# Running sums of squares on GpSimd instead of VectorE, in a decoder layer

## The reference

```python
def rms_norm(x, g):
    y = xf * lax.rsqrt(jnp.mean(xf * xf, axis=-1, keepdims=True) + EPS)
    return (y * g.astype(jnp.float32)).astype(x.dtype)

x = x + rms_norm(mix @ p["w_out"], p["g_post_mix"])
h = rms_norm(x, p["g_pre_x"])
qx = (h @ p["w_xq"]).reshape(B, T, N_XHEADS, XHEAD_DIM)
...
x = x + rms_norm(ox @ p["w_xo"], p["g_post_x"])
h = rms_norm(x, p["g_pre_ffn"])
...
x = x + rms_norm(f @ p["w_down"], p["g_post_ffn"])
```

## Time and profile before

| | |
|---|---|
| device time, median of 3 | 1866.59 us (1866.09 to 1868.44) |
| profiled execution, span | 1869.1 us (no other time of it is given) |
| PE / PEld busy | 94% / 87% |
| DVE / ACT / POOL busy | 61% / 47% / 0% |
| adds of Sy (line 2016) | 63, median 525 ns |
| adds of Sx (line 2023) | 42, median 518 ns |
| ACT's squares SQx waiting for the add of Sx | 27.8 us, 13 times |
| PE waiting for the add of Sx | 7.3 us, 3 times |

### The profile page before, as it was taken

The page is one execution under the profiler, slowest core; times in us unless marked ns, Lnnn a source line. Parts: engine busy times, 40 slices in busy tenths (PEclk is TensorE's granted clock), DMA queues, the critical chain, the costliest instruction groups (busy, mean ns, idle before and its releaser), DMA issues.

```text
span 1869.1 us, 30727 instructions
## 1 busy us (share of the span) xinstructions
PE 1761.3 (94%) x12286; PEld 1628.3 (87%) x12286; DVE 1133.8 (61%) x2091; ACT 875.7 (47%) x1648; POOL 0.9 (0%) x10
## 2 busy tenths in 40 slices
PE   7999999788997788999999899999999999999998
PEld 7999999455655688998877889999999999999998
DVE  5499993454674667743446766764467543576633
ACT  7322231233567465654545645543454543555533
POOL 0000000000000000000000000000000000000000
PEclk9999999899999899999999999999999999999999
DMA  7232122334322154544353333444444544444543
GB/s 236 57 121 80 59 92 92 142 119 159 120 78 93 49 159 129 158 149 128 121 156 115 100 114 115 137 140 133 141 136 141 156 132 139 139 137 144 148 137 102
DMA packets 349220, 233.76 MB, mean 125 GB/s; under 512 B 7979, under 2 KB 322465, under 8 KB 349071
## 3 DMA queue, kind: packets, MB, share of 16 engines
q1 hardware_dynamic: 342907, 220.24, 39.0%
q10 hardware_dynamic: 6172, 11.55, 1.7%
HBM read 220.68 MB, written 11.50 MB: 124 GB/s over the span
## 4 chain that ended last, share of the span: by engine, by line
PE 83%; DVE 8%; ACT 6%; issue 3%; DMA 1%; ACTq 0%; SPq 0%; DVEq 0%
PE bank L1144 77%; PE bank L1141 6%; DVE wlo L1721 1%; ACT whi L574 1%; DVE op_lo L1708 1%; DVE Y L1708 1%; DVE XT L2035 1%; ACT wide L588 1%; DVE Sx L2023 1%; ACT KTS L730 0%; ACT Pp L753 0%; DVE op_x L2038 0%; DMA cached<-in_cache_win_v_dram 0%; DVE KTS L1907 0%; DVE Sy L2016 0%
## 5 line engine op out<-in xcount | busy, mean ns | idle before, releaser
L1144 PE MATMUL bank<-op_hi,whi 128*128 128x352 f32 x1632 | 543.1, 333 | 21.7 <-DVE op_lo L1708 16.6
L1144 PE MATMUL bank<-op_hi,wlo 128*128 128x352 f32 x1632 | 528.6, 324 | 0.0
L1144 PE MATMUL bank<-op_lo,whi 128*128 128x352 f32 x1632 | 528.1, 324 | 0.0
L1721 DVE TENSOR_TENSOR wlo<-raw,whi 128x1024 fp32r<-128x1024 f32 (+1 forms) x312 | 373.3, 1199 | 245.8 <-ACT whi L574 245.2
L574 ACT ACTIVATE whi<-raw 128x1024 fp32r<-128x1024 f32 (+1 forms) x312 | 324.9, 1044 | 291.4 <-PE bank L1144 104.2
L1144 PEld LDWEIGHTS bank<-op_hi,whi 128*128 128x128 f32 x1632 | 310.5, 190 | 32.1 <-issue 26.2
L1144 PEld LDWEIGHTS bank<-op_lo,whi 128*128 128x128 f32 x1632 | 311.4, 191 | 0.5
L1144 PEld LDWEIGHTS bank<-op_hi,wlo 128*128 128x128 f32 x1632 | 310.1, 190 | 0.0
L1144 PE MATMUL bank<-fhi,whi 128*128 128x352 f32 x528 | 171.1, 324 | 0.0
L1144 PE MATMUL bank<-fhi,wlo 128*128 128x352 f32 x528 | 170.7, 323 | 0.0
L1144 PE MATMUL bank<-h1hi,whi 128*128 128x352 f32 x480 | 157.0, 327 | 3.0 <-DVE h1lo L1708 3.0
(11 more groups left out here) (277 smaller groups left out, 2369.2 us busy)
## 6 DMA issues: line engine op xcount, KB each, us to landing
raw<-in_w_up_dram SPq DMA_DIRECT2D x132, 512.0 KB, 3.8
raw<-in_w_down_dram SPq DMA_DIRECT2D x48, 512.0 KB, 3.6
raw<-in_w_out_dram SPq DMA_DIRECT2D x24, 512.0 KB, 3.7
raw<-in_w_xq_dram SPq DMA_DIRECT2D x24, 512.0 KB, 3.7
raw<-in_w_xo_dram SPq DMA_DIRECT2D x24, 512.0 KB, 3.7
raw<-in_w_in_dram SPq DMA_DIRECT2D x20, 512.0 KB, 3.8
raw<-in_w_down_dram SPq DMA_DIRECT2D x24, 384.0 KB, 3.2
cached<-in_cache_win_k_dram SPq DMA_DIRECT2D x8, 1024.0 KB, 5.4
```

The costliest lines, as they stand in the source:

```text
L1144: return pe.matmul(out, lhsT, rhs, start=first, stop=last)
L1721: dve.tensor_tensor(wlo[v % SLOTS][:, 0:nk, :], raw[v % SLOTS][:, 0:nk, :], whi[v % SLOTS][:, 0:nk, :].bitcast(F32), ALU.subtract).then_in ...
```

## The change

Both helpers move from VectorE's program to GpSimd's, with the waits and marks they have. GpSimd runs through the slots and issues in each first the add of Sy and then the adds of Sx. The places in VectorE's order where they stood are dropped.

```diff
     @block.gpsimd
@@ -559,6 +559,37 @@
         pool.memset(U[:, :, 0:PAD], 0.0).then_inc(*mark("pads", 0))
+
+        def add_y(name, c, m):
+            if m:
+                pool.wait_ge(*at("sqy", (name, c, m)))
+                if m > 1:
+                    pool.wait_ge(*at("ysum", (name, c, m - 1)))
+                pool.tensor_tensor(Sy[:, :], Sy[:, :], SQy[:, :], ALU.add).then_inc(*mark("ysum", (name, c, m)))
+
+        def add_x(name, c, m):
+            if m:
+                pool.wait_ge(*at("sqx", (name, c, m)))
+                if m > 1:
+                    pool.wait_ge(*at("xsum", (name, c, m - 1)))
+                pool.tensor_tensor(Sx[:, :], Sx[:, :], SQx[m % 2][:, :], ALU.add).then_inc(*mark("xsum", (name, c, m)))
+
+        def x_sums(t):
+            for name, c, s0, per, *_ in CHAINS:
+                for m in tiles(t - s0, 11, per):
+                    add_x(name, c, m)
+
+        for t in range(NX):
+            name, c, m = XU[t]
+            if name != "xq":
+                add_y(name, c, m)
+            x_sums(t)
+        for c in range(CH):
+            if c == 0:
+                for t in range(NX, NX + 2 * FT):
+                    x_sums(t)
+            for m in range(NT):
+                add_y("down", c, m)
@@ -2008,20 +2039,6 @@
-        def add_y(name, c, m):
-        ...
-        def add_x(name, c, m):
-        ...
@@ -2064,8 +2081,6 @@
         def chains_last(t):
             for name, c, s0, per, to, op_at, per_op in CHAINS:
-                for m in tiles(t - s0, 11, per):
-                    add_x(name, c, m)
@@ -2134,8 +2149,6 @@
-            if name != "xq":
-                add_y(name, c, m)
@@ -2230,7 +2243,6 @@
-                add_y("down", c, m)
```

## The result

The changed kernel takes 1880.7 us (median of 4 runs, 1879.2 to 1882.9) against 1867.5 us for the kernel before (4 runs too, one more than above): a ratio of 1.0065 (95% interval 1.0052 to 1.0077), or +12.1 us by the ratio. In the runs further down one execution of 4473 us and one of 3464 us were in a slow state and are left out. The profiled execution spans 1881.1 us, 12.0 more than before.

The account below looks back on a forecast made before the run. TensorE bounds most of the kernel, VectorE four stretches where it is about 96% full. Terms +11.8 - 0.8 + 0.4 = +11.4 us on 1866.6 gave 1878.0 us, range 1849 to 1892; slower 0.56, faster 0.34, same 0.10.

Parts of the forecast that it names:

- Part 1: Four stretches with VectorE about 96% full: removing 36 adds gives back 0.44 us each, 15.8 us; elsewhere nothing.
- the first rival: Whole kernel: GpSimd and VectorE don't disturb each other, so TensorE's stalls nearly all go; -19.7 us, 1847 us; chance 0.26.
- Part 2: On GpSimd: an add of 352 columns lasts 0.9 us, one stream at a time; at the top 1.2 us.
- Part 3: VectorE's two-operand instructions in the four nearly full stretches: each GpSimd add holds VectorE up its whole 0.9 us.
- Part 4: Four stretches with VectorE about 96% full: +16.6 us of hold, -4.8 us for ScalarE's earlier squares, together +11.8 us.
- Part 5: 1090 to 1130 us: seven adds cost +3.2 us, the 4.00 us stall before Sx goes; net -0.8 us, wlo late next.
- Part 6: Kernel's end: the last add of Sy, before the last roots, takes 0.9 us for 0.53, +0.4 us.
- Part 7: ScalarE's waits for sums from GpSimd's in-order queue: cost nothing unless an add takes over 1.3 us.
- the second rival: VectorE held only partly, 0.45 to 0.75 us an add, balance at 0.64: 1859 to 1872 us; chance 0.17.
- third rival: GpSimd too slow for its queue, over 1.3 us an add: about 10 us more, around 1877 and slower; chance 0.05.
- The signs: Adds of 0.9 us; VectorE instructions about 0.9 us longer, busy time up; XT and Y stalls +3 us each, 4.00 gone.

Follow-up runs that it names:

- One column on GpSimd: Changed kernel with each GpSimd add cut from 352 columns to one, same waits and order; 0.9907 against the kernel before, -17 us (1851.5 us).
- the extra adds: Kernel before, VectorE keeping its 105 adds, plus 105 same-size adds on GpSimd that nobody waits for; 1.0119 against the kernel before, +22 us.
- the third tile of squares: Kernel before with a third tile for squares of the residual, ScalarE waiting for sum m - 3 instead of m - 2; 0.9992, -1.5 us.
- writing-only kernel: Changed kernel with each GpSimd add replaced by three memsets, nothing read; 0.9952 against the kernel before, -9 us (1859.4 us).

## Why the prediction was right, point by point

The sign and the place are as forecast, and so is the mechanism in kind; 1878.0 lies 2.7 us from 1880.7, and +11.4 us beside +12.1. But the sum came out through errors that cancel. The hold and the credit were mis-sized and the price of the later sums was missing, so that it came this close is luck.

**Part 1, what comes back.** Right. One column on GpSimd, which takes the adds off VectorE at almost no price, gives -17 us; the first rival said -19.7.

**Part 2, the duration.** 0.9 us from the memsets' slope, 0.92 measured. But the reasoning isn't borne out. A memset of 352 columns took 0.39 us (0.37 by the slope), but a copy 0.48, where one stream at a time would give 0.64. For an add of one column, 176 and 352 the runs show 0.19, 0.55 and 0.92: 0.19 us and 2.08 ns a column, not 0.10 us and 3 x 0.77. The figure of the Trainium skill ("GPSIMD Engine Reference", section 3.1), scaled down in proportion to 0.77 us, came out too low because of the fixed 0.19. With it and the measured slope an estimate for 2048 columns is 4.45 us, close to the 4.50 that the page gives.

**Part 3, the hold.** Right in kind, shown by the extra adds (+22 us) and by the memsets (nothing lengthened). Mis-sized: taken as the whole 0.9 us, it measured 0.69 for one instruction. In the fourth stretch the means of VectorE's instructions in the changed kernel were these (line, name, count, busy us, mean ns):

```profile
L1752 DVE TENSOR_TENSOR wlo<-raw,whi 128x1024 fp32r<-128x1024 f32 x6 | 7.8, 1296 | 4.4 <-ACT whi L605 4.4
L1739 DVE SCALAR_TENSOR_TENSOR op_lo<-op_x,prm,op_hi 128x352 fp32r<-128x352 f32 x8 | 6.4, 834 | 0.0
L1739 DVE SCALAR_TENSOR_TENSOR Y<-Y,prm,Ry 128x352 f32<-128x352 f32 x8 | 6.0, 748 | 0.0
L2055 DVE TENSOR_TENSOR op_x<-XT,Rx 128x352 f32<-128x352 f32 x6 | 5.9, 1019 | 0.0
```

Before they were 1214, 577, 576 and 518 ns (the window of 1041 to 1070). The lengthening is 6 x 0.08 + 8 x 0.26 + 8 x 0.17 + 6 x 0.50 = 6.9 us for the 14 adds there. The same count gives 6.1, 5.7 and 5.1 us for the 9, 9 and 7 adds of the other three, together 23.8 us for 39 adds, 0.61 us each. Five of the 39 held nothing.

**Part 4, the sum of the full stretches.** The first term was 36 x (0.9 - 0.44) = +16.6 us; with 0.61 it is about +6. The credit of -4.8 us for ScalarE's earlier squares is wrong: the third tile of squares, which gives most of that freedom (10.8 of 27.8 us of waits for Sx stay), brought -1.5 us. ScalarE waits for XT instead.

**Part 5, the fifth stretch.** -0.8 us was forecast, and alone it measured 0.9997 (-2.4 to +1.1 us). The number holds, the reasons don't. The hold was put at 7 x 0.46 = +3.2 us, but there, in the changed kernel, VectorE's instructions grew by only 0.8 us in total for seven adds: four of these adds took 2.0 us, as a wlo got in ahead of them, and held the next wlo by only 0.19 us each. And the stall of 4.00 us doesn't go but splits in two; the new one stands behind ScalarE's root, not at wlo.

**Part 6, the end.** Only read, not tested alone: the last add took 0.93 us for 0.53, and TensorE's wait for it grew from 1.25 to 1.69 us. The down projections with all their adds moved measured no change.

**Part 7, the new waits.** This step failed, and its error makes up for those of parts 3 and 4. It said that the later sums cost nothing unless an add takes over 1.3 us. It took every add as 0.9 us, but the hold works on GpSimd too: the 42 adds of Sx took 1.35 us in the mean. And later sums cost something below that limit as well. The writing-only kernel disturbs VectorE in nothing and is still 8 us slower than the one of one column (0.9952 against 0.9907), its sums coming after 1.18 instead of 0.19 us. At the end of a chain nothing follows that could hide them: TensorE wants Sx at once, and in the changed kernel GpSimd had three adds to do, of 0.96, 0.92 and 1.72 us (1072.57 to 1076.28). There it waits 5.70 us where it waited 1.51.

The stall isn't the whole price. These windows of the writing-only kernel and of the one with one column run from the same instruction of TensorE to the same one, across one end of a chain (columns as in the earlier trace rows):

```profile
1030.68:1070.26 39.58, 33.38 (x196) 32.86 (x195) 25.66 (x44) 23.53 (x48) 15.27 (x42) 0.91 0.36 107
...
1027.16:1061.05 33.89, 30.72 (x196) 29.95 (x195) 25.66 (x44) 23.31 (x48) 5.11 (x14) 1.00 0.43 124
```

They differ by 5.7 us. One main part is the stall of 3.57 us. The other is the clock: it was granted at 1.00 throughout in the second, and at 0.91 in the first, 0.66 in the 10 us from 1056, that is partly at the lower of its two levels; for the same products TensorE is busy 2.7 us longer. The prediction has such a price in its first rival and none in its sum.

Put together from the runs: -17 us for adds taken off VectorE, +8 us for later sums, +21 us for GpSimd's reading, sum +12. The three are the steps from one whole kernel to the next, so they must add up; only the extra adds are a measurement beside them. They don't split further: the run with the adds of Sx first took 4 us off one wait and changed the total by nothing that can be told.

**The rivals.** "The engines don't disturb each other" fell with the extra adds; its time was right for the kernel of one column. By its hold the changed kernel belongs to the second rival: 0.61 us a piece lies in its 0.45 to 0.75, a little below its balance of 0.64. But for such a hold it gave 1859 to 1872 us, and 1880.7 was measured, because later sums had no price in it and the credit of 4.8 us was too large. GpSimd's queue (third rival) was given its price only from 1.3 us an add; lateness costs earlier than that. (The upper end of the range, 1892, adds up to 1891.2.)

**The signs.** The add's 0.9 us and the longer instructions came as described: Y from 0.58 to 1.27 us, wlo from 1.22 to 1.97 at the most. Two signs failed. VectorE's busy time didn't rise but fell by 20.5 us, for outside the full stretches 69 adds went and few were replaced by a hold. And the stalls by XT and Y grew by 1.06, 1.50 and 0.88 us, not by some 3 us each. The largest growth, 4.2 us, came in front of Sx, where none was forecast.

## What to carry to other kernels

Before moving an elementwise step from VectorE to GpSimd, look whether VectorE is full where the step stands, and whether its neighbours there read two operands from the on-chip memory (below, one with a single operand was held too). If both are so, the step isn't taken away but exchanged: here 0.44 us given back for 0.6 to 0.7 us of hold. The write-only steps held nothing, and only their lateness cost time; a step that reads has to be short, here under some 0.6 us.

Price also who wants the result next: a slot of slack hides a longer add in mid-chain, but not the last one. And a stall that ends is a gain only if nothing behind it in the chain was waiting anyway.

## What the runs showed of the hardware

The two engines took turns rather than slowing each other. A held VectorE instruction of 352 columns ended 0.38 us after GpSimd's add, at full and at half width, and 0.37 us after a copy. That makes it longer by less than GpSimd's instruction lasts: 0.69 us for 0.92, and 0.21 for a copy of 0.48. It is mutual: of the 37 adds of the changed kernel that took over 1.04 us, 36 ended 0.78 to 0.81 us after a two-operand instruction of VectorE, which makes them last up to 2.0 us where that instruction is a wlo. A single read stream on GpSimd suffices, and memsets of 352 columns back to back leave VectorE's durations at 0.53 and 0.58 us. With one operand VectorE's instructions go both ways. Timeline of VectorE of the changed kernel:

```profile
639.43 2.35 DVE L2026 RECIPROCAL RSCA<-STDA 128x352 f32<-128x352 f32 x1 [1.79 <-ACT STDA L836]
...
937.33 0.89 DVE L2145 TENSOR_SCALAR Pm<-Pm,rden 128x256 f32<-128x256 f32 x1
...
941.58 0.35 DVE L2105 TENSOR_SCALAR PX<-PX,rden 128x256 f32<-128x256 f32 x1
```

And GpSimd's adds beside the first two:

```profile
639.83 0.96 POOL L568 TENSOR_TENSOR Sy<-Sy,SQy 128x352 f32<-128x352 f32 x1 [6.20 <-ACT SQy L865]
...
937.14 0.93 POOL L568 TENSOR_TENSOR Sy<-Sy,SQy 128x352 f32<-128x352 f32 x1 [4.41 <-ACT SQy L865]
```

The reciprocal takes 2.35 us, as its like do without an add, and the add inside it 0.96: neither notices the other. The scaling of Pm met an add and took 0.89 us, where one of the same shape with GpSimd idle takes 0.35. So one operand alone doesn't decide it, and what tells these two apart was not tested here.
